# Three chained blocks on one core: block 1's head projections in rounded parts split by GpSimd, two norms moved, block 3's heads two at a time

## The reference, cut to what matters

```
h = rms_norm(h_res, norm_mix_w)
p_rwkv, p_diff, p_gate = split(h @ w_in)
o_rwkv = rwkv7_mix(p_rwkv, ...) @ rwkv_w_o
o_diff = diff_attention(p_diff, ...) @ diff_w_o
gates = sigmoid(p_gate)
h_res = h_res + (gates[0] * o_rwkv + gates[1] * o_diff) @ w_out
h_res = h_res + square(relu(rms_norm(h_res, norm_mlp_w) @ mlp_w1)) @ mlp_w2
out = rms_norm(h_res, final_norm_w)[:, 16:]
```

## Time and profile before

| | |
|---|---|
| median of 3 runs | 4041.95 us (4035.01 to 4048.01) |
| the profiled execution | 4039.47 us, span 4037.7 us, mean granted clock 0.899 |
| TensorE busy | 3594.5 us, 89% of the span, 29006 matmul records |
| VectorE | 1621.2 us, 40% |
| ScalarE | 1196.8 us, 30% |
| GpSimd | 153.8 us, 4%, 117 instructions |
| chain that ended last | TensorE 77%, VectorE 10%, ScalarE 9% |
| DMA | 236.23 MB, mean 59 GB/s |

### The profile page before, as it was taken

The page is one execution under the profiler, slowest core; times in us unless marked ns, Lnnn a source line. Parts: engine busy times, 40 slices in busy tenths (PEclk is TensorE's granted clock), DMA queues, the critical chain, the costliest instruction groups (busy, mean ns, idle before and its releaser), DMA issues.

```text
span 4037.7 us, 66990 instructions
## 1 busy us (share of the span) xinstructions
PE 3594.5 (89%) x29006; PEld 2789.7 (69%) x29006; DVE 1621.2 (40%) x2901; ACT 1196.8 (30%) x1990; POOL 153.8 (4%) x117
## 2 busy tenths in 40 slices
PE   7888898889879989998788878888999999888998
PEld 6666676667669979996666666666778776444444
DVE  2443434343425344344445345565542444322121
ACT  2323322322222222222434455432222222223330
POOL 0000000000002110000011001110000000000000
PEclk9889898889759989998888889899899999978887
DMA  3001010001003223331111112132233232200111
GB/s 124 23 25 30 20 29 29 20 28 31 20 9 118 78 93 92 92 90 54 52 50 60 46 56 68 54 122 81 66 89 94 89 89 78 84 16 27 41 37 37
DMA packets 63590, 236.23 MB, mean 59 GB/s; under 512 B 7232, under 2 KB 7232, under 8 KB 62144
## 3 DMA queue, kind: packets, MB, share of 16 engines
q1 hardware_dynamic: 57168, 209.16, 17.1%
q0 software_dynamic: 2672, 16.50, 1.1%
q10 hardware_dynamic: 3456, 6.29, 0.4%
HBM read 219.28 MB, written 12.65 MB: 57 GB/s over the span
## 4 chain that ended last, share of the span: by engine, by line
PE 77%; DVE 10%; ACT 9%; issue 3%; DMA 1%; POOL 0%; ACTq 0%; DVEq 0%; SPq 0%; POOLq 0%
PE psum L405 75%; ACT arena L326 5%; DVE arena L341 4%; ACT arena L334 3%; DVE arena L350 2%; PE psum L409 1%; ACT L322 1%; DVE ring L341 1%; DVE arena L345 1%; ACT L326 1%; DVE arena L353 1%; DMA ring<-in_w 1%; DVE arena L362 0%; DVE arena L368 0%; DVE arena L365 0%
## 5 line engine op out<-in xcount | busy, mean ns | idle before, releaser
L405 PE MATMUL psum<-arena,ring 128*128 128x264 f32 (+2 forms) x5304 | 1626.1, 393 | 7.0 <-DVE arena L350 6.2
L405 PE MATMUL psum<-arena,arena 128*128 128x264 f32 (+1 forms) x6288 | 1525.2, 346 | 63.3 <-DVE ring L341 20.5
L405 PE MATMUL psum<-arena 32*32 32x32 f32 (+16 forms) x16392 | 1120.0, 247 | 327.3 <-DVE arena L341 84.7
L405 PEld LDWEIGHTS psum<-arena 32*32 32x32 f32 (+10 forms) x16392 | 786.6, 138 | 681.0 <-issue 324.2
L405 PEld LDWEIGHTS psum<-arena,arena 128*128 128x128 f32 x6288 | 1035.3, 193 | 229.8 <-issue 55.2
L405 PEld LDWEIGHTS psum<-arena,ring 128*128 128x128 f32 (+1 forms) x5304 | 964.2, 196 | 255.4 <-issue 128.7
L334 ACT ACTIVATE arena<-psum 128x512 f32<-128x512 f32 (+12 forms) x625 | 282.3, 452 | 1000.9 <-PE psum L405 884.3
L341 DVE TENSOR_TENSOR ring<-ring,arena 128x1024 fp32r<-128x1024 f32 (+1 forms) x301 | 360.5, 1198 | 487.5 <-ACT arena L334 482.8
L341 DVE TENSOR_TENSOR arena<-arena 128x528 f32<-128x528 f32 (+9 forms) x692 | 331.0, 478 | 373.6 <-ACT arena L326 231.7
L334 ACT ACTIVATE arena<-ring 128x1024 fp32r<-128x1024 f32 (+1 forms) x301 | 308.8, 1026 | 536.3 <-PE psum L405 472.0
L341 DVE TENSOR_TENSOR arena<-arena,psum 88x192 f32<-88x192 f32 (+4 forms) x428 | 193.4, 452 | 565.9 <-PE psum L405 555.0
(11 more groups left out here) (35 smaller groups left out, 637.8 us busy)
## 6 DMA issues: line engine op xcount, KB each, us to landing
ring<-in_w SPq DMA_DIRECT2D x368, 512.0 KB, 3.5
bg<-arena ACTq DMA_DIRECT2D x24, 256.0 KB, 2.0
ring<-in_w SPq DMA_DIRECT2D x24, 256.0 KB, 2.6
arena<-in_x SPq DMA_DIRECT2D x2, 2112.0 KB, 11.5
arena<-bg POOLq DMA_DIRECT2D x1, 3072.0 KB, 17.9
od<-arena POOLq DMA_DIRECT2D x8, 264.0 KB, 2.3
arena<-od POOLq DMA_DIRECT2D x1, 2112.0 KB, 9.0
out<-arena SPq DMA_DIRECT2D x1, 2048.0 KB, 6.3
```

Source lines behind the costliest of these rows:

```text
L405: self.last_ins = self.eng.matmul(out, l, r, start=start, stop=stop, skip_group_check=skip)
```

## The change

Block 1, projections of the heads. `m.h` is split in parts at the start (`m.hh_r`, rounded, by ScalarE; `m.h_r`, low, by VectorE, in place). The 51 slabs come in halves of 512 columns, one a ring place, and GpSimd splits each inside its place. Halves are multiplied by `mm3`.

```diff
+def pe_half(K, run, off):
+    P, i = K.P, len(run.offs)
+    run.offs.append((off, HALF))
+    n, raw = P.slab(off, "slab", run.name, i, size=HALF)
+    P.wait_ge(*K.book.at("lo", run.name, i))
+    lo, hi = K.halves[n % RING]
+def pool_half(K, run):
+    n, raw, _ = raw_of(K, run, i)
+    lo, hi = K.halves[n % RING]
+    G.wait_ge(*landed(K, n))
+    G.cp(hi[:], raw)
+    G.tt(lo[:], raw, hi[:], SUB, "lo", run.name, i)
...
     def prep(hp):
         for i, nme in enumerate("rkv"):
-            s, w = P.slab((3 + 3 * hp + i) * SLAB, "rw_proj", hp, i)
-            for k in range(8):
-                for j in range(2):
-                    P.mm(ps[...], w[:, k, :], m.h[...], k == 0, k == 7)
-                if k % 2 and k < 7:
-                    yield
+            for half in range(2):
+                wh, wl, done = pe_half(K, m.wr, (3 + 3 * hp + i) * SLAB + half * HALF)
+                for k in range(4):
+                    pe_terms(K, m, b, wh(k), wl(k), 4 * half + k)
+                    if k == 1:
+                        yield
+                P.did(*done)
...
+                if half == 0:
+                    yield
```

```diff
+def pool_heads(K, m, oy, od):
+    for taken, what, i in m.wr.after:
+        while m.wr.lows < min(taken + 3, len(m.wr.offs)):
+            pool_half(K, m.wr)
+        if what == "od":
+            G.wait_ge(*at("df_od", i))
+            G.eng.dma_start(od[:, S], m.df.t1)...
+        else:
+            G.wait_ge(*at("rw_out", i))
+            G.eng.dma_start(oy[:, S], m.fin[0])...
```

```diff
+    for k in range(2):
+        for g in range(2):
+            for half in range(2):
+                wh, wl, done = pe_half(K, m.wr, (59 + 3 * k + g) * SLAB + half * HALF)
+                for kk in range(4):
+                    pe_terms(K, m, b, wh(kk), wl(kk), 4 * half + kk)
...
+                P.advance_both()
     P.drain()
```

```diff
+def act_widened(K, m, k):
+    A.wait_ge(*K.book.at("hres", k))
+    A.copy(m.hh_r[k][:], xs, "h2_hi", k, scale=K.p["nmlp"][:, k:k + 1])
+    A.act(m.odh[:, k * T:k * T + T], xs, ACT.Square, "sq", "mlp", k)
+def dve_widened(K, m, k):
+    V.stt(m.h_r[k][:], m.orw[...], K.p["nmlp"][:, k:k + 1], m.hh_r[k][:], MUL, SUB, "h2_low", k)
 def pe_mlp(K, m):
-    pe_sum8(K, "mlp", m.Hh, T)
...
             i += 1
+            if i == 2:
+                pe_sum8(K, "mlp", m.odh, T)
...
+            V.stt(h2(m.rl[k % 2]), out_of(K, 2, T, "relu", half, k), 0.0, h2(m.rs2), MAX, MUL, "relu", half, k)
```

```diff
+            if half:
+                for kk in (k - 1,) if k < 7 else (6, 7):
...
+                        P.mm(K.ps[...bs...], K.c["ones"], m.sqx[:, S], kk == 0, kk == 7)
+                        P.mm(K.ps[...bm...], K.c["ones"], m.out[:, S], kk == 0, kk == 7)
-    pe_sum8(K, "fin", m.oy, T)
...
+    dve_centre(K, "ln0", m.x, T)
+    V.stt(m.rs, out_of(K, 1, T, "root", "ln0"), 1.0 / 1024, m.floor, MUL, ADD, "spread")
+    for k in range(9):
+        if k < 8:
+            V.stt(xs, xs, K.p["ln0_g"][:, k:k + 1], m.rs, MUL, MUL, "ln0_g", k)
+        if k:
+            V.wait_ge(*at("ln0_hi", k - 1))
+            V.stt(m.h_r[k - 1][:], m.x[...], K.p["ln0_b"][...], m.hh_r[k - 1][:], ADD, SUB, "normed", "ln0", k - 1)
```

```diff
-        def scores(r, i):
+        def scores(i):
+            s_ = [bk(P.bank(1, "fx_e", t, r, i))[:, 0:W] for r in range(2)]
+            for r, R in enumerate(R2):
+                P.mm(s_[r], d.q[R, J4[i]], d.k[R, 128 * k0:128 * (i + 1)], True, False)
...
             for j in range(W // 128):
-                P.mm(bk(bo)[64 * r:64 * r + 64, J4[i]], V[:, v0:v0 + 64], d.t[i % 2][:, J4[j]], ...)
+                for r, R in enumerate(R2):
+                    P.mm(bk(bo)[R, J4[i]], V[:, v0:v0 + 64], d.t[2 * (i % 2) + r][:, J4[j]], ...)
...
-        for r in range(2):
-            for i in range(4):
-                scores(r, i)
+        for i in range(4):
+            scores(i)
```

More of the change, by code:

```diff
@@ L309, in advance, with advance_both @@
                 self.work.pop(0)
+    def advance_both(self):
+        self.advance()
+        if not self.work:
+            next(self.beside, None)
     def drain(self):
@@ L682, in memory1 @@
     m.base = M.top
-    m.oy, m.h = M(8 * T), M(8 * T)
+    m.hh, m.h = M(8 * T), M(8 * T)
+    m.hh_r, m.h_r = M.rounded(m.hh, T), M.rounded(m.h, T)
+    m.wr = Run(K, "heads", [], [])
     m.mark = M.top
@@ L998, in pe_rwkv @@
         P.work.append(f)
+    for k in range(2):
+        for g in range(2):
+            b = P.bank(2, "gate", g, k)
+            P.keep(b, 2)
+            for half in range(2):
+                wh, wl, done = pe_half(K, m.wr, (59 + 3 * k + g) * SLAB + half * HALF)
+                for kk in range(4):
+                    pe_terms(K, m, b, wh(kk), wl(kk), 4 * half + kk)
+                P.did(*done)
+                if half:
+                    P.also("gate_lin", g, k)
+                    P.drop(b, 2)
+                P.advance_both()
     P.drain()
@@ L1007, in act_rwkv @@
     A, at, ps, p, T = K.A, K.book.at, K.ps, K.p, T1
-    A.wait_ge(*at("normed", "mix", 7))
+    for k in range(8):
+        A.wait_ge(*at("normed", "mix", k))
+        A.copy(m.hh_r[k][:], m.h[:, k * T:k * T + T], "h_hi", k)
     A.wait_ge(*at("shz"))
@@ L1123, in act_rwkv @@
         A.work.append(f)
+    for k in range(2):
+        for g in range(2):
+            A.advance_both()
+            A.advance_both()
+            act_gate(K, m, g, k)
     A.drain()
@@ L1302, in dve_rwkv @@
         V.work.append(f)
+    for _ in range(8):
+        V.advance_both()
     V.drain()
@@ L1719, in dve_mlp @@
                 dve_next(K, m.wm, i)
+                if k == 0 and g == 0:
+                    dve_hidden(K, m, half, 15)
                 i += 1
@@ L2927, in pe_block2 @@
     K.P.wait_ge(*K.book.at("con_late"))
-    K.P.colsum(("mean", "ln0"), ("centred", "ln0", 7), K.c["ones"], [m.x[:, k * T2:(k + 1) * T2] for k in range(8)], T2, [("normed", "fin", k) for k in range(8)])
     pe_sum8(K, "ln0", m.O, T2)
@@ L3079, in values @@
+            P.did("fx_s", t, i)
+        def values(i):
+            k0, W = keys_of(kind, i)
+            for r in range(2):
+                P.wait_ge(*at("fx_p", t, r, i))
+                b = P.bank(1, "fx_a", t, r, i)
+                for j in range(W // 128):
+                    P.tr(bk(b)[:, J4[j]], d.P[2 * (i % 2) + r][:, J4[j]])
+                P.did("fx_tr", t, r, i)
             yield
-            P.wait_ge(*at("fx_a", t, r, i))
+            P.wait_ge(*at("fx_a", t, 0, i))
+            P.wait_ge(*at("fx_a", t, 1, i))
@@ L3467, in layout_engines @@
     K.ring_r = K.mem.rounded(ring[:, :], SLAB)
+    half = K.mem.rounded(ring[:, :], HALF)
+    K.halves = [half[2 * n:2 * n + 2] for n in range(RING)]
     K.c, K.p = {}, {}
```

422 lines of the change are left out of this document (247 added, 175 removed).

## The result

The changed kernel takes 3912.3 us in the median of 4 runs (3906.6 to 3921.2), the kernel before, on the same chip, 4038.5 us (4034.5 to 4048.0). The ratio is 0.9686, 95% interval 0.9659 to 0.9713: 126 us less, where 109 were forecast. Two further comparisons of the same two kernels gave 0.9723 (0.9707 to 0.9738) and 0.9718 (0.9688 to 0.9748), 111 and 113 us less: the changed kernel took 3912 to 3914 us in all three, the kernel before 4023 and 4026 in the later two. The profiled execution took 3914.9 us, its span is 3913.0, against 4037.7 before.

A forecast was written before the change was run, and what follows sets the result against it. TensorE was taken to bound the whole span, with holes from waits on VectorE and ScalarE. Terms 43 + 7 - 12 + 8 + 23 + 7 + 33 = 109 us from 4039.5 gave 3931, range 3885 to 3990.

The forecast's parts named there:

- Heads, 43 less 12: Block 1's heads: projections in rounded parts save 43 us (20 to 72); GpSimd delaying VectorE costs 12 (0 to 39).
- 60% of 72: Heads: projections shrink 19%, 72 us of TensorE work; 60% leaves the span, as shortened fillers before holes only lengthen them.
- Rival (c): TensorE's clock in heads and tail: more short idle time brings more low clock, gain shrinks 20 us, 3950; chance 0.14.
- VectorE is on the path in about a third of the stage: Heads: of 39 us that VectorE waits for GpSimd, about a third reaches the path, price 12 us.
- Start, 7: Start of the heads: projections save 11.6 us, the first slab ends about 4.5 later; net 7 less (2 to 12).
- Tail and gates, 8: Heads' tail to output projection: four gate slabs moved in, oy through DRAM; 8 us less (loss of 4 to gain of 15).
- with those steps TensorE finishes near 1225: Heads' tail: four gate slabs, 23.5 us, laid between the last pair's closing steps, are done by about 1225 us.
- MLP's factor, 23 less 10.7: MLP: factor applied at the eviction saves 23 us (15 to 25); six pairs of sums moved inside add 10.7.
- Final norm and layer norm in one, 17.7 in the joint: Joint to block 2: 7 us net (2 to 12) plus 10.7 of sums moved into the MLP; centring ends at 1873.
- Block 3, 33: Block 3's attention, heads in twos: 33 us less (10 to 60); score overlap 20, alternating value products up to 10.
- 24 steps instead of 48: Block 3: fewer steps wait for the chain of maximum, exponential, copy; no size of its own within the 33 us.
- Rival (d): The parts carry more: heads 72 us, block 3 55; kernel at 3885; chance 0.12.

The follow-up runs named there:

- Plain heads: Changed kernel with one plain f32 product per weight part, not three rounded, in heads and four gate slabs: 3940.3 us, 0.9787 of the kernel before.
- two terms: Changed kernel without the product of low weight part and high activation part in heads and four gate slabs: 3884.0 us, 0.9643 of the kernel before.
- Gates back: Changed kernel with the four gate slabs returned to the gates stage, parts made by ScalarE and VectorE: 3922.5 us, 0.9734 of the kernel before.
- early load: Changed kernel with oy and od loads and first gate weight parts ahead of the waits for the heads' ends: 3902.8 us, 0.9698 of the kernel before.
- centre first: Changed kernel with two weight parts moved behind squares and centring in the joint to block 2: 3913.0 us, 0.9727 of the kernel before.

## Why the prediction was right, point by point

The forecast was 3931 with a range of 3885 to 3990 and 0.88 on faster; 3912 lies inside and the sign is right. The sum came out close partly because errors cancelled.

- **Heads, 43 less 12.** The net of 31 met 27.2 in the first pair of traces, and here the errors cancelled. Plain heads puts the rounded products at 20 to 31 us in the heads, not 43, and shows no price of GpSimd where 12 was taken off. The yield of 60% of 72 failed twice. The 19% that the group was to lose would have been 70 us of its 369.5 in this stretch; it lost 47.2. Of these, 11.9 went into the other matmuls, dearer at the lower clock, and 8.1 into idle time. The reason given for the missing 40%, holes, was the smaller part; two terms shows the clock taking it. How much of the 23 us by which the group itself fell short is the clock stays open: the mean clock of the stretch, 0.82 for 0.84, makes some 7. Rival (c), the clock, named that mechanism and priced it at 20 us.
- **GpSimd.** Copy 0.8 estimated, 0.66 measured. VectorE does meet it (708 to 761 ns, then 786 with twice the copies), as the Trainium skill (GPSIMD Engine Reference, Key points) says of instructions with two SBUF inputs. The prediction put the delay at 39 us and a third of it on the path. The delay was 19 us in plain heads, and of a share of it on the path nothing can be seen. The failed step is "VectorE is on the path in about a third of the stage".
- **Start, 7.** 6.2 measured, and both of its terms hold: 11.6 less 4.5 forecast, 10.5 less 4.3 by plain heads (114.41 - 103.92 and 114.41 - 110.12).
- **Tail and gates, 8.** 1.0 measured. The step that failed is "with those steps TensorE finishes near 1225", 29 us behind the last sum at 1196.0. It took 35.7 (1162.64 to 1198.3): the closing steps are matmuls for 10.6 of their 13.1 us, and the four slabs took 27.1 us and not 23.5, the first half of one 5.65 where 2.94 was taken. The wait behind them, for oy's load, its rounding and subtraction, was 9.45 us where the forecast had 8. It begins so late because the load is issued at 1199.6, when all three engines have ended. Gates back shows the first, early load the second.
- **MLP's factor, 23 less 10.7.** 11.9 of 12.3, and here the two terms were right each. TensorE stood idle for 13.7 us of this stretch before (403.95 less 390.29 busy) and for 0.0 after, and the sums that moved into it are 11.9 us, as the row below says (1424.62 to 1816.65 after). No run took this part alone.

```profile
L410 PE MATMUL psum<-arena 128*128 128x512 f32 x25 | 11.9, 591 | 0.0
```

- **Final norm and layer norm in one, 17.7 in the joint.** 11.5 measured. The step "centring 1873" overlooked two weight parts that stand ahead of the centring on VectorE; centre first gives 5 of the 6 back.
- **Block 3, 33.** 63 measured, the largest miss. The score overlap of 20 was right in kind and a little small (29 us of the stage; the score groups of 256 and 512 columns alone fell from 38.8 to 23.1 us). The up to 10 for alternating value products is nothing. The term that was mis-sized is the steps: "24 steps instead of 48" got no figure of its own, the 33 leave it 3 to 13, and it is 38 by subtraction. Most of it, 23.4 us, is busy time of TensorE and not the waits that the prediction named. Rival (d) had 55 for this stage, but with 72 in the heads. The sign "near 460" was for a window of 495 us; the window that answers to it is the 432.7 above.
- **Block 2, 0.** 5.3 less in the first trace; the repeats of the change and of kernels with the same code there run from 1533 to 1544, so this is spread.
- **Sums.** Rival (d)'s terms give 3880 and not 3885, and the forecast against the median is 3933 and not 3932; neither changes a reading. The total came close partly by luck: in the table, block 3's 30 us too few stand against 17 too many in heads, tail and joint.

## What to carry to other kernels

Work taken out of a TensorE stream with holes in it comes back partly as a lower clock, so busy time alone overstates the gain: two terms paid about 30 us where the group's busy time fell by 67, and the idle share, 13.8% to 14.9% of the stretch, did not announce the fall from 0.82 to 0.75. Running two heads in one step was worth more, 38 us, than making their score products overlap, 29. And work laid ahead of a load hides it only if the load's issue does not itself wait for that work.

## What the runs showed that was not expected

- Identical code in the heads ended between 1151.7 and 1163.3 us over ten runs. The difference is TensorE's busy time, 901 to 916 us for the same 14980 records, and not its idle time, 141 to 147; the granted clock is 0.83 in the three shortest stretches and 0.81 or 0.82 in the others. No run held the clock fixed, so the clock is the likeliest cause and not a shown one.
- Side by side on different row halves, a score product of 256 columns cost 0.25 us a record (12.0 / 48), apart 0.43 (20.7 / 48), while value products on different column halves showed 22.8 us alternating and 25.0 in series.
- The load of oy goes out as two halves of 1056 KB each, half a us apart, and 7.8 us is the median of the two: the first landed after 6.8, the second after 8.8. So all of oy was there 9.3 us after its first issue, about what the same 2112 KB of od took before, 9.0. The prediction's 5 us for half the size did not come, with the second half under way beside the first. od, queued behind them, took 13.3.

```profile
arena<-oy POOLq DMA_DIRECT2D x2, 1056.0 KB, 7.8
```
